# First block of a two-block model: gate columns taken with the index key, values projected by feature, and a 16-token gather tile padded to 128 rows

## The reference, cut to what matters

```python
for l in range(DEPTH):
    proj = h @ w_in[l]
    dq, dk, dv, dz, db, da, sq, sk, sv, iq, ik, iw = jnp.split(proj, SPLIT_POINTS, axis=-1)
    o_dn = deltanet_group(dq, dk, dv, dz, db, da, conv_w[l], a_log[l], dt_bias[l], dn_norm_g[l])
    o_sa = dsa_group(sq, sk, sv, iq, ik, iw, cos, sin, cos_i, sin_i, k_top)
    mix = jnp.concatenate([o_dn, o_sa.astype(o_dn.dtype)], axis=-1) @ w_out[l]
    h = layer_norm(DEEPNORM_ALPHA * h + mix, ln1_g[l], ln1_b[l])
    ffn = hier_moe(h, w_grp[l], b_grp[l], w_rtr[l], b_rtr[l], w1[l], w3[l], w2[l])
    h = layer_norm(DEEPNORM_ALPHA * h + ffn, ln2_g[l], ln2_b[l])
```

## Time and profile before

| | |
|---|---|
| median of 3 runs | 2472.61 us |
| profiled execution, its span | 2475.7 us, 2473.9 us |
| TensorE (PE) busy | 2269.3 us, 92% |
| VectorE (DVE) busy | 837.0 us, 34% |
| ScalarE (ACT) busy | 513.2 us, 21% |
| GpSimd (POOL) busy | 53.9 us, 2% |
| mean granted TensorE clock | 0.953 |
| DMA | 426.67 MB, mean 172 GB/s |

### The profile page before, as it was taken

One profiled execution on the slowest core, in us unless ns is written; L12 is line 12 of the kernel. 1 busy time (PEld: TensorE's weight loads), 2 busy tenths in 40 slices (PEclk: granted clock), 3 DMA queues, 4 the chain that ended last, 5 costly groups with the idle time before them and its releaser, 6 DMA issues. The chain is left out here.

```text
span 2473.9 us, 33836 instructions
## 1 busy us (share of the span) xinstructions
PE 2269.3 (92%) x12870; PEld 1724.1 (70%) x12870; DVE 837.0 (34%) x1877; ACT 513.2 (21%) x1174; POOL 53.9 (2%) x28
## 2 busy tenths in 40 slices
PE   8998899886999889988699999999999999999999
PEld 6766766543876766544575777888877677788887
DVE  3465233232456324223335333211122532321112
ACT  2213320002312331000333422010012243201000
POOL 0120000000021000000000000000000000000000
PEclk9889889998988998999899999999999999999999
DMA  7220249996321063999654134333345403343433
GB/s 228 80 87 35 103 170 378 425 425 240 113 87 44 35 272 146 419 425 420 224 136 145 35 137 136 137 137 136 136 159 137 145 34 137 102 140 135 168 136 119
DMA packets 165171, 426.67 MB, mean 172 GB/s; under 512 B 40409, under 2 KB 54294, under 8 KB 140454
## 3 DMA queue, kind: packets, MB, share of 16 engines
q1 hardware_dynamic: 165030, 424.80, 46.6%
HBM read 419.06 MB, written 1.05 MB: 170 GB/s over the span
## 5 line engine op out<-in xcount | busy, mean ns | idle before, releaser
L2061 PE MATMUL bank<-hT,W 128*128 128x256 f32 (+1 forms) x1440 | 329.5, 385 | 6.9 <-ACT b_gates L2189 5.9
L2061 PEld LDWEIGHTS bank<-hT,W 128*128 128x128 f32 (+1 forms) x1440 | 269.4, 190 | 53.0 <-issue 12.3
L261 PE MATMUL bank<-hT,W 128*128 128x272 f32 x928 | 247.6, 427 | 16.8 <-issue 11.7
L261 PEld LDWEIGHTS bank<-hT,W 128*128 128x128 f32 x928 | 191.3, 209 | 65.9 <-issue 23.3
L3038 PE MATMUL bank<-hT,W 128*128 128x256 f32 x1024 | 225.5, 381 | 6.7 <-DVEq L3095 6.7
L3054 PE MATMUL bank<-u_hid,W 128*128 128x256 f32 x1024 | 223.3, 379 | 0.0
L3038 PEld LDWEIGHTS bank<-hT,W 128*128 128x128 f32 x1024 | 195.6, 191 | 34.3 <-issue 7.4
L3054 PEld LDWEIGHTS bank<-u_hid,W 128*128 128x128 f32 x1024 | 194.6, 190 | 26.5
L1320 PE MATMUL bank<-e_sel,rowsH 128*128 128x128 f32 (+1 forms) x768 | 149.4, 328 | 0.0
L1434 PE MATMUL bank<-W,e_hs 128*32 128x256 f32 x1792 | 112.3, 409 | 32.3 <-DMA W<-in_w 29.8
L1320 PEld LDWEIGHTS bank<-e_sel,rowsH 128*128 128x128 f32 (+1 forms) x768 | 113.9, 204 | 37.2 <-issue 11.6
(11 more groups left out here) (555 smaller groups left out, 2784.4 us busy)
## 6 DMA issues: line engine op xcount, KB each, us to landing
W<-in_w SPq DMA_DIRECT2D x112, 1024.0 KB, 16.7
W<-in_w_in SPq DMA_DIRECT2D x41, 2048.0 KB, 8.1
e_Wd<-in_w SPq DMA_DIRECT2D x64, 1024.0 KB, 12.6
W<-in_w_up SPq DMA_DIRECT2D x16, 2048.0 KB, 8.4
W<-in_w_down SPq DMA_DIRECT2D x16, 2048.0 KB, 7.9
W<-in_w_out SPq DMA_DIRECT2D x8, 2048.0 KB, 8.2
e_w_ahead<-in_w SPq DMA_DIRECT2D x16, 1024.0 KB, 15.9
W<-in_mem_w_kv SPq DMA_DIRECT2D x6, 2048.0 KB, 10.3
```

The costliest lines, as they stand in the source:

```text
L261: mm = nc.tensor.matmul(bank[:, 0:T], w[:, k, c0:c0 + P], m.hT[:, k, :], **st)
L2061: mm = nc.tensor.matmul(o[0:n, 0:S2], w[:, k, a:a + n], m.hT[:, k, :], start=(k == 0), stop=(k == KT - 1))
```

## The change

There are three edits.

1. *Gates with the index key.* The chunk "in8" now holds 80 columns (`ik`, `iw`, `db`, `da`) instead of 144. One product by feature gives `ik` in rows 0 to 63 and the 16 gate rows in 64 to 79. ScalarE copies both parts out; the gate rows are turned into token rows by three transposes on TensorE, which stand behind the first `iq` product, and VectorE copies them in six pieces, since their order is changed. The index key is no longer produced twice; a fifth DMA copies its 64 rows to the upper half, and GpSimd waits for that one too.
2. *Values by feature.* `sv` is projected by feature in four products, copied to `svT` (which lies in z's buffer), and turned by 12 transposes into the same three banks that the token-wise products filled before. `projection_time` changes with it, so that the z products come one place earlier, and the mixing order moves.
3. *Padded gather tile.* The gather multiplies all 128 rows of the 16-token tile; rows 16 to 127 of `rowsH` are set to zero once a layer by GpSimd, and ScalarE waits for that before it copies rows.

```diff
 def projection_time(n):
 
-    if n < 12:
+    if n < 14:
         return 4.0 * n
-    if n < 15:
-        return 48.0 + 2.0 * (n - 12)
-    if n < 28:
-        return 54.0 + 4.0 * (n - 15)
...
+    if n < 27:
+        return 52.2 if n == 14 else 56.0 + 4.0 * (n - 15)
...
-    plan += [("bai", "in8", 0, j) for j in range(3)]
-    plan += [("rope", "in8", 16, 0)]
-    plan += [("rope", "in7", 128 * j, 1 + j) for j in range(4)]
+    plan += [("rope", "in8", 0, 0)]
+    plan += [("rope", "in7", 0, 1), ("bai", "in8", 0, 0)]
+    plan += [("rope", "in7", 128 * j, 1 + j) for j in range(1, 4)]
     plan += [("rope", "in4", 128 * j, 5 + j) for j in range(4)]
     plan += [("rope", "in5", 128 * j, 9 + j) for j in range(4)]
+    plan += [("value", "in6", 128 * j, j) for j in range(4)]
     plan += [("sv", "in6", 0, j) for j in range(3)]
     plan += [("z", "in3", 128 * j, j) for j in range(4)]
...
-                sp.dma_start(w[:, :, 0:8], w_in[l, :, :, 2048:2056]).then_inc(done, 16)
-                sp.dma_start(w[:, :, 8:16], w_in[l, :, :, 4168:4176]).then_inc(done, 16)
-                sp.dma_start(w[:, :, 16:80], w_in[l, :, :, 4104:4168]).then_inc(done, 16)
-                sp.dma_start(w[:, :, 80:144], w_in[l, :, :, 4104:4168]).then_inc(done, 16)
+                sp.dma_start(w[:, :, 0:72], w_in[l, :, :, 4104:4176]).then_inc(done, 16)
+                sp.dma_start(w[:, :, 72:80], w_in[l, :, :, 2048:2056]).then_inc(done, 16)
...
+            if r == 0:
+                sp.dma_start(x[64:128, :, :], x[0:64, :, :]).then_inc(S["rope_swapped"], 16)
...
+            if kind == "bai":
+                pe.wait_ge(S["bai_sb"], 1)
+                for c, (t0, nt) in enumerate(TILES):
+                    mm = nc.tensor.transpose(bank[0:nt, 16 * c:16 * c + 16], m.baiT[64:80, t0:t0 + nt], m.ident[64:80, 64:80])
+            elif kind == "sv":
+                t0, nt = TILES[idx]
+                for j in range(4):
+                    pe.wait_ge(S["value_sb"], j + 1)
+                    mm = nc.tensor.transpose(bank[0:nt, j * P:(j + 1) * P], m.svT[:, j, t0:t0 + nt], m.ident[:, :])
+            else:
+                rows = 80 if chunk == "in8" else P
+                for k in range(KT):
+                    mm = nc.tensor.matmul(bank[0:rows, 0:T], w[:, k, c0:c0 + rows], m.hT[:, k, :], start=(k == 0), stop=(k == KT - 1))
...
+                elif chunk == "in8":
+                    nc.scalar.activation(m.baiT[64:80, :], src[64:80, 0:T], ACT.Copy).then_inc(S["bai_sb"], 1)
+                    nc.scalar.activation(m.ikT[0:64, :], src[0:64, 0:T], ACT.Copy).then_inc(S["proj_by_act"], 1)
+                    act.drain().then_inc(S["rope_in"], 1)
...
+                elif kind == "value":
+                    nc.scalar.activation(m.svT[:, idx, :], src[:, 0:T], ACT.Copy).then_inc(S["proj_by_act"], 1)
+                    act.drain().then_inc(S["value_sb"], 1)
...
-                nt = TILES[idx][1]
-                nc.vector.tensor_copy(m.bai[0:nt, idx, :], ps[n % 2][0:nt, 0:16])
+                for c, (t0, nt) in enumerate(TILES):
+                    turned_bai = ps[n % 2][0:nt, 16 * c:16 * c + 16]
+                    nc.vector.tensor_copy(m.bai[0:nt, c, 0:8], turned_bai[:, 8:16])
+                    nc.vector.tensor_copy(m.bai[0:nt, c, 8:16], turned_bai[:, 0:8])
...
+                nc.gpsimd.memset(m.rowsH[:, 0, :], 0.0)
+                pool.drain().then_inc(S["r_padded"], 1)
...
+                act.wait_ge(S["r_padded"], 1)
...
-        for c, (t0, nt) in enumerate(TILES):
-            mm = nc.tensor.matmul(o, m.rowsH[0:nt, c, d * P:(d + 1) * P], m.sel[0:nt, c, :], start=(c == 0), stop=(c == 2))
+        for c in range(3):
+            mm = nc.tensor.matmul(o, m.rowsH[:, c, d * P:(d + 1) * P], m.sel[:, c, :], start=(c == 0), stop=(c == 2))
```

More of the change, by code:

```diff
@@ L251, in on_tensor @@
             bank = ps[n % 2]
-            for k in range(KT):
-                st = dict(start=(k == 0), stop=(k == KT - 1))
-                if kind == "sv":
-                    t0, nt = TILES[idx]
-                    mm = nc.tensor.matmul(bank[0:nt, 0:512], m.hT[:, k, t0:t0 + nt], w[:, k, :], **st)
-                elif kind == "bai":
-                    t0, nt = TILES[idx]
-                    mm = nc.tensor.matmul(bank[0:nt, 0:16], m.hT[:, k, t0:t0 + nt], w[:, k, 0:16], **st)
-                else:
-                    mm = nc.tensor.matmul(bank[:, 0:T], w[:, k, c0:c0 + P], m.hT[:, k, :], **st)
+            if kind == "bai":
[11 more added lines that the diff above has]
+                    mm = nc.tensor.matmul(bank[0:rows, 0:T], w[:, k, c0:c0 + rows], m.hT[:, k, :], start=(k == 0), stop=(k == KT - 1))
             mm.then_inc(S["proj"], 1)
@@ L548, in chunk_on_scalar @@
         if c == 2:
[L549 removed]
+            yield max(end_time(c, 4), projection_time(37) + 4)
             act.drain()
@@ L1713, in first_block @@
         for name, slot in CHUNK_SLOTS:
-            ring.add(name, slot, dmas=4 if name == "in8" else int(name not in ("in0", "in1", "in2")))
+            ring.add(name, slot, dmas=2 if name == "in8" else int(name not in ("in0", "in1", "in2")))
         signals = {name: sem(name) for name in SEMS1}
```

31 lines of the change are left out of this document (17 added, 14 removed).

## The result

The changed kernel takes 2445.87 us (median of 4 runs, 2443.45 to 2446.40) against 2472.60 for the kernel before on the same chip; the ratio of the runs is 0.9891, 95% interval 0.9874 to 0.9908. It is 1.1% faster. The profiled execution took 2445.36 us, with a span of 2443.5 us and a mean granted clock of 0.953, the same as before.

The account below looks back on a forecast made before the run. Mixing was taken as bound by TensorE together with VectorE and ScalarE chains, the experts by the weights' DMA stream. Experts -9.5 and mixing -4 us, times 2 layers, give -27 us: 2445.6 us, range 2420 to 2465.

Parts of the forecast that it names:

- Padded gather: Experts' stage: a gather of 8.35 us loses 3.0 us, the price of 16 row changes at 0.19 us each.
- Rival B: Experts' stage: rows don't matter, the gather stays as it is and the experts give nothing; 2464.6 us; 5%.
- First gather: Start of the experts' stage, before the weight stream: padded, 15.3 us become 9.3, so -6.0 us a layer.
- First expert product: Experts' stage: it runs at the full clock, 7.1 instead of 8.72 us; its first half gives -1.5 us.
- The hole in the DMA stream: Experts' stage, at the second gather: the gather's saving comes off the hole, -3.0 us; longer waits may cost +1.0.
- Rival D: Experts' stage: all eight gathers of a layer gain, another -18 us a layer; 2409.6 us; 2%.
- The gates: Mixing: 7.6 us of TensorE work saved, mostly eaten by 4.5 us idle before the second iq product; net -1.8, taken -1.
- rival C: Slower: new waits, low clock and a held mask lengthen mixing by 12.5 us a layer; 2478.6 us; 6%.
- The holds by GpSimd: Mixing: rotations move relative to VectorE, some holds go and others come; -1 us, between -4 and +5.
- The values: Mixing: 4.1 us less TensorE work, counted as -3; +2 us at the layer's end for the moved z product.
- Mixing in sum: Mixing: terms of -3 us, and -1 for a clock that falls less often: -4 us a layer, bounds +7 and -17.
- Rival A: Mixing is bound by TensorE after all: -13 us a layer there, 2427.6 us; 22%.

Follow-up runs that it names:

- e_neighbours: The kernel before, still unpadded, with the gather's 16-row products of neighbouring feature tiles placed next to each other; 2467.71 us, ratio 0.9988.
- e_pad: The kernel before with the gather's 16-token tile padded to 128 rows and nothing else; 2451.81 us, ratio 0.9921.
- e_pad_first: The kernel before with the 16-token tile padded only in the first of a layer's eight gathers; 2457.08 us, ratio 0.9967.
- e_values: The kernel before with only the values edit: sparse values projected by feature in four products and turned; 2452.71 us, ratio 0.9928.
- e_spare2: The kernel before, unpadded, with five more spare 512-column products in the route, ahead of the first gather; 2454.86 us, ratio 0.9924.
- e_pad_rest: The kernel before with the 16-token tile padded only in the seven later gathers of a layer; 2467.41 us, ratio 0.9985.
- e_act: The changed kernel with ScalarE's gate exponentials put behind its copy of the first index-query product; 2432.95 us, ratio 0.9859 to the kernel before.
- e_unpad2: The changed kernel without its padding, gates and values as changed; 2471.11 us, ratio 1.0004 to the kernel before.
- e_gates: The kernel before with only the gates edit: gate columns share the index key's product; 2478.49 us, ratio 1.0031.
- e_both2: The changed kernel with ScalarE's copy ahead of the gates' exponentials and GpSimd's third rotation held until the rank mask; 2429.15 us, ratio 0.9823 to the kernel before.

## Why the prediction was right, and where it was right by luck

The total, 2445.6 us, came true to 0.3 us, and the forecast's mechanism for the experts held. The terms did less well than their sum: padding brought more than its part and mixing less, and that the two errors cancelled to 0.3 us is luck.

*Padded gather.* Foretold 5.35 us, measured 5.36. The price was put on the change of rows, 0.19 us each, and the records of e_neighbours show 0.19. Rival B (rows don't matter) falls with that. The Trainium skill ("TensorE: Matmul & The Clock Gate", the summary table) says rows don't change a product's time. For products of equal rows the trace agrees (0.11 us a record on 16 rows and on 128); for products that alternate, the measurement decides against it.

*First gather.* Foretold 9.3 us, measured 7.6 (changed kernel) and 8.6 to 8.8 (e_pad, e_pad_first). That the clock returns within a padded gather, which the forecast took on trust, is borne out by the count above: it came back in 0 of 11 unpadded and 11 of 11 padded ones. Why it does is not shown. What the prediction missed is that 15.3 us was not a property of the kernel before: at the full clock the unpadded gather takes 8.7 us (e_values, both layers; e_spare2, layer one). The term of -6.0 measured -7.7 in the profile, or -6.5 with this edit alone. *First expert product*: -1.5 foretold, 8.72 to 7.11 us measured, and W1's issue 1.6 us nearer to its start. Together the stream starts 9.3 us earlier, where 7.5 were foretold.

*The hole in the DMA stream.* Foretold -3.0 us a layer, less 1.0 for longer waits, so -2.0. The issue did move 3.1 us nearer (24.64 to 21.58 us). Of that the changed kernel paid back 1.1 us in layer one and 2.4 in layer two (9.3 + 3.1 against 11.3 and 10.0). With this part alone, the stage gained 1.0 and 1.1 us in e_pad_rest and 2.0 and 1.4 between e_pad_first and e_pad. So the term was right in kind, and the +1.0 was up to 1.4 us too small: in e_pad_rest the stage has 14.5 us more of waiting for weights and 19 us more at the low clock. Rival D (all gathers pay) is refuted: 1 us of 21.

Together the experts' terms were -9.5; with all three edits it measured -11.3 and -10.0.

*The gates.* The wait for ScalarE's copy was foretold at 4.5 us and measured 4.37, with ScalarE named. Its cost was too small in the prediction: the first chunk product was to come at 94.1 and came at 96.74. The difference is the low clock after the wait, +2.5 us, which the text named ("if the 4.5 us idle brings the clock down for one projection, the gain is gone") and for which it then took only 0.8 (-1 in place of -1.8); in full it stands in rival C alone. Undoing the wait (e_act) brought 12.6 to 12.9 us by the medians, about 6.4 a layer; the wait shortened by 4.0 and the projection by 2.3, 6.3 in all, and the mixing stages by 5.6 and 6.4 against the first profile.

*The holds by GpSimd.* Foretold -1 within -4 and +5. The kind was right, the place was not: one hold went (2.58 to 0.43 us) and two in a row came (2.97 and 2.78 us). Rival C's "caught mask" did happen, at the rotation of sq instead of iq.

*The values.* Foretold -3 for the work and +2 at the layer's end. The total of e_values cannot size it, since the gather's clock carries much of that. The work itself shrank as foretold: three products of 6.87 us in the kernel before (the expectation of e_values has 5.8 to 6, which is wrong), four of about 3.7 and 12 transposes of 1.4 us in all after. An estimate: within one code, the mixing stage of layer two took 271.8 us with 50 us at the low clock (the kernel before) and 260.5 with 25 us (e_spare2); a line through all 12 stages of that code gives 0.43 us for each us at the low clock, and they scatter by 1.6 us about it. By that line e_values's mixing is 2.6 and 4.6 us shorter. At the layer's end the wait that the moved z product no longer fills is 1.14 us (265.60, for VectorE), where 1.7 were taken.

*Mixing in sum.* Foretold -4 a layer; the one profile showed -4.4 and -6.2 and seemed to agree. It does not stand. Over the 12 mixing stages profiled with the code of before, the mean is 268.9 us (260.5 to 273.1), over the 6 with both edits 267.7 (265.0 to 270.9), and e_unpad2 against the kernel before gives no difference, with an interval of about 5 us either way. So mixing brings about 1 us a layer and can't be told from nothing. The term of -4 was mis-sized. Two parts of it came out otherwise: the low clock behind the foretold wait (+2.5 us, of which 0.8 were taken), and the holds by GpSimd, taken as -1, behind which TensorE now waits 4.23 us and runs a projection at the lower clock. How the missing 3 us divide between them was not separated. The missing 3 us a layer were made up by the padding, which is worth 25.5 us (20 to 33) beside the other edits where I had 19. That surplus may be chance in part. What can be narrowed: in the kernel before, in e_gates and in e_unpad2, 6 of 6 first gathers took 14.7 us or more, and the changed kernel's four took 7.5 to 7.6. Of those 7.7 us the changes of rows make 2.7 at the full clock, so the clock makes most of it.

*Rival A* (mixing bound by TensorE, 13 us a layer) did not come. The two stalls took a part of it: with both removed, e_both2's mixing of 263.3 and 259.9 us is some 7 us a layer below the mean of the code before, so about half of A was there to be had.

## What to carry to other kernels

Keep the operand shapes of a run of small products equal where padding is free: it saves each change, and in the first gathers of these runs the clock came back after it fell only where the operands were equal. When a product is moved ahead, look in the list of the engine that empties its bank for what stands before that copy; a wait of 4 us for a table load and a chain costs its own length and, as here, can bring a projection at half the clock. And before a gain is given to an edit by comparing two profiles, look how far the same stage, with the same code, differs between layers and runs; here it was 12.6 us in a stage where the edits were worth about 1.

## What the runs showed that I had not expected

- One stage at one code (mixing) took from 260.5 to 273.1 us, and goes with the time at the low clock; the kernel's total moves with the mean granted clock, 2447.9 us at 0.967 and 2478.3 at 0.951 on one chip.
- The clock can fall with TensorE without a gap: at full clock and busy for 6.00 of 6 us (916 to 922 in e_spare2), it fell inside the alternating gather and stayed at 1.2 GHz to the end of it. What took it down is not shown.
- With five idle-filling products more in each layer (e_spare2) the kernel was 16 us faster; the gathers explain part of it, the rest stands in mixing and is unexplained.
- The second block, with its code the same in every run, took 1270.6 to 1276.8 us over the profiles, the longest beside the gates' edit alone (e_gates). One profile doesn't show that the edit did it.
